# Delta rule with two pairs' token halves exchanged, and SSM decays as one product of 512 columns

## The reference

```python
def step(s, inp):
    r_t, w_t, k_t, v_t, kk_t, a_t = inp
    sa = jnp.einsum('bhvk,bhk->bhv', s, -kk_t)
    s = (s * w_t[:, :, None, :] + sa[..., None] * (kk_t * a_t)[:, :, None, :]
         + v_t[..., None] * k_t[:, :, None, :])
    return s, jnp.einsum('bhvk,bhk->bhv', s, r_t)
```

```python
a_cum = jnp.cumsum(dt * a.reshape(G, hg), axis=2)
seg = a_cum[:, :, :, None] - a_cum[:, :, None]
lmat = jnp.exp(jnp.where(mask, seg, -jnp.inf))
y_diag = jnp.einsum('bcqsgh,bcsghp->bcqghp', cb[..., None] * lmat, xdt)
```

## Time and profile before

| | |
|---|---|
| median of 3 runs | 3658.43 us |
| the profiled execution | 3661.18 us |
| its span, first to last instruction | 3659.9 us |
| TensorE busy, matmul / weight load | 3473.9 us (95%) / 2884.4 us (79%) |
| VectorE busy | 2100.5 us (57%) |
| ScalarE busy | 1330.3 us (36%) |
| mean granted TensorE clock | 0.976 |
| matmul records | 23320 |

### The profile page before, as it was taken

The page is one execution under the profiler, slowest core; times in us unless marked ns, Lnnn a source line. Parts: engine busy times, 40 slices in busy tenths (PEclk is TensorE's granted clock), DMA queues, the critical chain, the costliest instruction groups (busy, mean ns, idle before and its releaser), DMA issues.

```text
span 3659.9 us, 55917 instructions
## 1 busy us (share of the span) xinstructions
PE 3473.9 (95%) x23320; PEld 2884.4 (79%) x23320; DVE 2100.5 (57%) x3889; ACT 1330.3 (36%) x2454; POOL 65.0 (2%) x32
## 2 busy tenths in 40 slices
PE   7999999999999999999999988998999989889999
PEld 6777688788888777788788877786888778778887
DVE  6777643543457776535544467754655589573434
ACT  4456443342234555433332222222322234232222
POOL 0000000000000000000000000000000033000000
PEclk9999999999999999999999989999999999889999
DMA  4221223233333221233333332234100324233332
GB/s 133 81 62 50 58 76 110 81 99 97 98 125 92 74 61 52 64 97 100 88 97 98 104 89 73 83 95 137 29 29 21 116 70 135 84 115 92 98 98 87
DMA packets 353826, 315.36 MB, mean 86 GB/s; under 512 B 11348, under 2 KB 281812, under 8 KB 353576
## 3 DMA queue, kind: packets, MB, share of 16 engines
q1 hardware_dynamic: 352712, 309.56, 28.3%
q10 hardware_dynamic: 864, 2.23, 0.2%
HBM read 288.15 MB, written 23.59 MB: 85 GB/s over the span
## 4 chain that ended last, share of the span: by engine, by line
PE 77%; DVE 15%; ACT 5%; issue 3%; DMA 1%; POOL 0%; DVEq 0%; ACTq 0%; SPq 0%; POOLq 0%
PE banks L508 12%; PE banks L510 12%; PE banks L509 12%; PE banks L411 8%; PE banks L413 8%; PE banks L412 8%; PE banks L2578 6%; DVE weights_r L352 2%; PE banks L3000 2%; PE banks L608 1%; ACT weights_high_r L345 1%; PE banks L1091 1%; PE banks L1078 1%; ACT probabilities L1227 1%; DVE softmax_stats L1259 1%
## 5 line engine op out<-in xcount | busy, mean ns | idle before, releaser
L352 DVE TENSOR_TENSOR weights_r<-weights,weights_high_r 128x1024 fp32r<-128x1024 f32 (+3 forms) x520 | 606.6, 1174 | 478.5 <-ACT weights_high_r L345 477.8
L508 PE MATMUL banks<-h_T_hi,weights_high_r 128*128 128x512 f32 (+2 forms) x1904 | 759.7, 399 | 29.9 <-DVE h_T_lo L855 15.2
L510 PE MATMUL banks<-h_T_hi,weights_r 128*128 128x512 f32 (+2 forms) x1904 | 738.0, 388 | 0.0
L509 PE MATMUL banks<-h_T_lo,weights_high_r 128*128 128x512 f32 (+2 forms) x1904 | 737.8, 387 | 0.0
L345 ACT ACTIVATE weights_high_r<-weights 128x1024 fp32r<-128x1024 f32 (+3 forms) x520 | 510.4, 992 | 388.8 <-DMA weights<-in_w_mlp 217.9
L508 PEld LDWEIGHTS banks<-h_T_hi,weights_high_r 128*128 128x128 f32 x1904 | 362.9, 191 | 116.1 <-issue 38.0
L510 PEld LDWEIGHTS banks<-h_T_hi,weights_r 128*128 128x128 f32 x1904 | 362.2, 190 | 72.0
L509 PEld LDWEIGHTS banks<-h_T_lo,weights_high_r 128*128 128x128 f32 x1904 | 363.2, 191 | 69.0 <-issue 3.2
L411 PE MATMUL banks<-weights_high_r,h_T_hi 128*128 128x512 f32 (+3 forms) x704 | 290.5, 413 | 13.1 <-DVE h_T_lo L855 9.4
L413 PE MATMUL banks<-weights_high_r,h_T_lo 128*128 128x512 f32 (+3 forms) x704 | 266.6, 379 | 0.0
L412 PE MATMUL banks<-weights_r,h_T_hi 128*128 128x512 f32 (+3 forms) x704 | 266.4, 378 | 0.0
(11 more groups left out here) (541 smaller groups left out, 5643.6 us busy)
## 6 DMA issues: line engine op xcount, KB each, us to landing
weights<-in_w_in SPq DMA_DIRECT2D x182, 512.0 KB, 3.8
weights<-in_w_mlp SPq DMA_DIRECT2D x128, 512.0 KB, 3.8
weights<-in_ffn_w_in SPq DMA_DIRECT2D x44, 512.0 KB, 3.8
weights<-in_w_out SPq DMA_DIRECT2D x24, 512.0 KB, 3.6
weights<-in_ffn_w_down SPq DMA_DIRECT2D x22, 512.0 KB, 3.3
weights<-in_w_mem_kv SPq DMA_DIRECT2D x16, 512.0 KB, 3.6
weights<-in_w_diff_o SPq DMA_DIRECT2D x16, 512.0 KB, 4.0
weights<-in_w_mla_o SPq DMA_DIRECT2D x8, 512.0 KB, 3.4
```

Source lines behind the costliest of these rows:

```text
L352: ve.e.tensor_tensor(self.part(c.w_raw_r, u), self.part(c.w_raw, u), self.part(c.w_high_r, u).bitcast(F32), ALU.subtract).then_inc(*ve.tel ...
L508: pe.e.matmul(out, lhsT=wh[:, k, :], rhs=hi[k][:, cols], start=(k == 0), stop=False)
L509: pe.e.matmul(out, lhsT=wh[:, k, :], rhs=lo[k][:, cols], start=False, stop=False)
L510: mm = pe.e.matmul(out, lhsT=wl[:, k, :], rhs=hi[k][:, cols], start=False, stop=(k == self.chunks - 1))
```

## The change

In the delta rule the two halves of pairs f = 2 and 3 are exchanged in all tiles whose rows are tokens (low, w, cut, the six further products' tiles, x and sa). A product between a feature tile and a token tile then goes from one half of the partitions to the other for these two pairs. Inside the levels `cut` and `w` are exchanged, `t` and `prod` are not, so `prod` and `w step` cross for pairs 2 and 3, and `t step` does not. The initial `t` is masked from a product of its own, "low t", and not from `low`. `multiply` stays for products that don't cross. `crossing` and `swapping` issue the pairs in the order 0, 2, 1, 3 and write pairs 0, 1 to one bank and pairs 2, 3 to another; `fill_two` hands out two banks of the ring with one mark for when they are free, and a bank that would part the two at the ring's end is kept for the next single product. Some products share two banks (low with w, bu with rb, vtok with btok). The six further products move from one in each half level to 2, 2, 1, 1 ahead of levels 1 to 4. x and y are split in a straight part and a crossing part that adds to it.

```diff
+    def crossing(self, name, n, d, *terms, start=True):
+        pe, (together, at, _) = self.c.pe, self.SHARED[name]
+        if at == 0 and (together, n, d) not in self.two:
+            self.two[(together, n, d)] = self.two_banks(together, n, d)
+        for f in (0, 2, 1, 3):
+            for k, (lhsT, rhs) in enumerate(terms):
+                for rows in range(2):
+                    own, other = (slice(x % 2 * RC, (x % 2 + 1) * RC) for x in (rows, rows + f // 2))
+                    right = rhs[own, :] if len(rhs.shape) == 2 else rhs[own, f, :]
+                    mm = pe.e.matmul(self.two[(together, n, d)][f // 2][other, (2 * at + f % 2) * RC:(2 * at + f % 2 + 1) * RC],
+                                     lhsT=lhsT[own, f, :], rhs=right, start=start and k == 0,
+                                     stop=k == len(terms) - 1 and (start or f % 2 == 1))
+        mm.then_inc(*pe.tell("filled", name, n, d))
+    def two_banks(self, *key):
+        c = self.c
+        if (c.turns["scans"] + 1) % 6 == 0:
+            self.spare.append(c.next_of("scans"))
+        return c.fill_two(*key, ring="scans")
...
         pe.wait_ge("scaled_key", n, d)
-        self.multiply(("low", n, d), (o["a"], u["b"]))
-        self.multiply(("w", n, d), (u["b"], o["a"]))
+        self.crossing("low", n, d, (o["a"], u["b"]))
+        self.crossing("w", n, d, (u["b"], o["a"]))
+        self.multiply(("low t", n, d), (o["a"], u["b"]))
         yield
         pe.wait_ge("scaled_all", n, d)
-        fill = [("bu", (u["k"], o["a"])), ("vtok", (self.v[:, :, tc], i64)), ("rb", (u["b"], o["r"])), ("btok", (u["b"], i64)),
-                ("rk", (u["k"], o["r"])), ("ktok", (u["k"], i64))]
+        more = {1: (("vtok", (self.v[:, :, tc], i64)), ("btok", (u["b"], i64))), 2: (("bu", (u["k"], o["a"])), ("rb", (u["b"], o["r"]))),
+                3: (("ktok", (u["k"], i64)),), 4: (("rk", (u["k"], o["r"])),)}
         for lev in range(1, 6):
-            if fill:
-                name, term = fill.pop(0)
-                self.multiply((name, n, d), term)
+            for name, term in more.get(lev, ()):
+                self.crossing(name, n, d, term)
             yield
             pe.wait_ge("cut", n, d, lev)
             pe.wait_ge("w_level", n, d, lev - 1)
-            self.multiply(("prod", n, d, lev), (u["cut"], o["w"]))
-            if fill:
-                name, term = fill.pop(0)
-                self.multiply((name, n, d), term)
+            self.swapping(("prod", n, d, lev), u["cut"], o["w"])
             yield
             pe.wait_ge("emptied", "prod", n, d, lev)
             pe.wait_ge("t_level", n, d, lev - 1)
-            self.multiply(("w step", n, d, lev), (u["t"], u["prod"]))
+            self.swapping(("w step", n, d, lev), u["t"], u["prod"])
             if lev < 5:
                 self.multiply(("t step", n, d, lev), (u["prod"], u["t"]))
...
+        self.straight("x", n, d, (o["bu"], o["vtok"]))
...
-        self.multiply(("x", n, d), (o["a"], u["z"]), (o["bu"], o["vtok"]))
+        pe.wait_ge("straight", "x", n, d)
+        self.crossing("x", n, d, (o["a"], u["z"]), start=False)
...
-        self.multiply(("state", n, d), (o["btok"], u["sa"]), (o["ktok"], o["vtok"]))
-        self.multiply(("y", n, d), (u["z"], o["r"]), (u["sa"], o["rb"]), (o["vtok"], o["rk"]))
+        self.crossing("state", n, d, (o["btok"], u["sa"]), (o["ktok"], o["vtok"]))
+        pe.wait_ge("straight", "y", n, d)
+        self.crossing("y", n, d, (u["sa"], o["rb"]), (o["vtok"], o["rk"]), start=False)
```

```diff
-            for j in range(4):
-                mm = pe.e.matmul(bank[:, j * P:(j + 1) * P], lhsT=u["lhs"][q % 2][:, j * P:(j + 1) * P], rhs=k.upto[d], start=True, stop=True)
-            mm.then_inc(*pe.tell("filled", "ssm decay", d, n, q))
+            pe.e.matmul(bank[:, :], lhsT=k.strict[d], rhs=u["terms"][q % 2], start=True, stop=True).then_inc(*pe.tell("filled", "ssm decay", d, n, q))
```

Three plan times move:

```diff
-        P_.beside(cross, 238.5, 284.5, 0.38)
+        P_.beside(cross, 238.25, 284.25, 0.38)
...
-        plan.beside(rule, plan.now + 18, plan.now + 63.24, 1.08)
+        plan.beside(rule, plan.now + 18, plan.now + 63.37, 1.02)
...
-        plan.at(FirstGates(merge_h), (plan.now - 2,))
+        plan.at(FirstGates(merge_h), (plan.now - 1.62,))
```

More of the change, by code:

```diff
@@ L2572, in multiply @@
         c, pe = self.c, self.c.pe
-        bank = c.fill(*key, ring="scans")
+        bank = c.fill(*key, bank=self.spare.pop(0) if self.spare else c.next_of("scans"))
         for f in range(self.pairs):
@@ new lines, in two_banks, with swapping @@
+    def two_banks(self, *key):
[3 more added lines that the diff above has]
+        return c.fill_two(*key, ring="scans")
+    def swapping(self, key, lhsT, rhs):
+        c, pe = self.c, self.c.pe
+        two = self.two_banks(*key)
+        for f in (0, 2, 1, 3):
+            for rows in range(2):
+                own, other = (slice(x % 2 * RC, (x % 2 + 1) * RC) for x in (rows, rows + f // 2))
+                mm = pe.e.matmul(two[f // 2][other, f % 2 * RC:(f % 2 + 1) * RC], lhsT=lhsT[own, f, :], rhs=rhs[own, f, :],
+                                 start=True, stop=True)
+        mm.then_inc(*pe.tell("filled", *key))
@@ new lines, in swapped, with straight @@
+    def swapped(self, *key):
+        return self.c.slots[key][:, :, 0:2 * RC].rearrange("p b (f s) -> p b f s", f=2)
+    def straight(self, name, n, d, *terms):
+        pe, (together, at, _) = self.c.pe, self.SHARED[name]
+        if at == 0 and (together, n, d) not in self.two:
+            self.two[(together, n, d)] = self.two_banks(together, n, d)
+        for f in range(self.pairs):
+            for k, (lhsT, rhs) in enumerate(terms):
+                for own in (slice(0, RC), slice(RC, P)):
+                    mm = pe.e.matmul(self.two[(together, n, d)][f // 2][own, (2 * at + f % 2) * RC:(2 * at + f % 2 + 1) * RC],
+                                     lhsT=lhsT[own, f, :], rhs=rhs[own, f, :], start=k == 0 and f % 2 == 0, stop=False)
+        mm.then_inc(*pe.tell("straight", name, n, d))
@@ new lines, in shared, with wait_taken, wait_written @@
+    def shared(self, name, n, d):
+        together, at, _ = self.SHARED[name]
+        return self.c.slots[(together, n, d)][:, :, 2 * at * RC:(2 * at + 2) * RC].rearrange("p b (f s) -> p b f s", f=2)
+    def wait_taken(self, lane, name, n, d):
+        together, _, last = self.SHARED[name]
+        lane.wait_ge(*(("emptied", together) if last else ("taken", name)), n, d)
+    def wait_written(self, lane, name, n, d):
+        lane.wait_ge("filled", {"low": "w", "bu": "rb", "vtok": "btok"}.get(name, name), n, d)
@@ L2582, in got, with halves, taken @@
+    def halves(self, x):
+        return x.rearrange("p (b f) s -> p b f s", b=2)
+    def taken(self, lane, name, n, d):
+        together, _, last = self.SHARED[name]
+        return lane.frees(together, n, d) if last else lane.tell("taken", name, n, d)
     def got(self, *key):
@@ L2629, in copy @@
                     ac.wait_ge("filled", "y", n - 2, d)
-                ac.e.activation(o[name], self.got(name, n, d), ACT.Copy).then_inc(*ac.frees(name, n, d))
+                ac.e.activation(self.halves(o[name]), self.shared(name, n, d), ACT.Copy).then_inc(*self.taken(ac, name, n, d))
         for lev in range(1, 6):
-            if fill:
-                copy(fill.pop(0))
+            for name in {1: ("vtok", "btok"), 3: ("ktok",)}.get(lev, ()):
+                copy(name)
             yield
@@ L2691, in prepare_dve @@
             ve.e.tensor_tensor(u["cut"], u["low"], wide(k.level64[1 - d][lev]), ALU.mult).then_inc(*ve.tell("cut", n, d, lev))
-            if fill:
-                mask(*fill.pop(0))
+            for what in masks.get(lev, ()):
+                mask(*what)
             yield
-            if fill:
-                mask(*fill.pop(0))
             yield
             ve.wait_ge("filled", "w step", n, d, lev)
-            ve.e.tensor_tensor(w, w, self.got("w step", n, d, lev), ALU.subtract).then_inc(*ve.frees("w step", n, d, lev))
+            ve.e.tensor_tensor(halves(w), halves(w), self.swapped("w step", n, d, lev), ALU.subtract).then_inc(*ve.frees("w step", n, d, lev))
             c.values[("w_level", n, d, lev)] = ve.end
```

80 lines of the change are left out of this document (47 added, 33 removed).

## The result

The changed kernel takes 3629.9 us (median of 4 runs, 3628.0 to 3632.8) where the kernel before took 3658.5 on the same chip: a ratio of 0.9916, 95% interval 0.9904 to 0.9928. That is 29 us faster; the forecast was 42. The profiled execution took 3631.3 us, its span is 3630.0.

A forecast was written before the change was run, and what follows sets the result against it. TensorE was taken to bound the delta rule's stage, though not by much. From the 3658.43 us median, 41 us off the rule (36 + 4.5 + 0.5) and 1 off the SSM decays gave 3616; range 3600 to 3672.

The forecast's parts named there:

- TensorE's share: Sign in the delta rule's stage: TensorE's busy share should fall from 94% to some 85%.
- the distance of x to x: Sign, one chunk of the delta rule: over 38 us would make the prediction wrong.
- The waits for the cut: Sign at the rule's matmuls: waits for VectorE's cut should rise from 11 us.
- Price of a crossing product: Delta rule on TensorE: 0.26 us instead of 0.467, about 0.39 a term with two terms; saves 60 us of TensorE.
- the lower bound: Delta rule on TensorE: all four corners in step, 0.234 us a term everywhere, saving 78 us of TensorE.
- The rival of serial loads: Delta rule on TensorE: loads of one row half go serially, price stays 0.467 us, kernel slower at 3671; chance 0.21.
- the floor on starts: TensorE: about 25 ns between starts, so no term under 0.40 us, result near 3650; no separate chance given.
- Chunk 0 and the end: Delta rule's ends: preparation of chunk 0 saves 4.5 us, the last step 0.5 us.
- Net 5.2 us of a 40 us chunk: Delta rule's chunks: saving left after 0.6 us given back to bank waits; seven chunks give 36 us.
- The granted clock: Delta rule's stage: half speed in a tenth of it, 14 us less work done, giving 3630; no separate chance given.
- SSM decays: SSM scan: 8 records of 128 columns become 2 of 512, saving 1 us, bounds -1.5 and +1.
- cross and FirstGates: Layers' cross attention and hgrn gates, issue times moved: only queue places change, taken at 0, bounds -2 and +5.

The follow-up runs named there:

- e7: Kernel after with the pairs of crossing products issued in order 0, 1, 2, 3 instead of 0, 2, 1, 3; ratio 0.9925 to the kernel before.
- the second profile: Profile of the kernel after, run again unchanged as a control; ratio 0.9913 to the kernel before, stage 288.4 us.
- e6: Kernel after with the three plan times of before (cross, the rule, FirstGates) put back; 3639.0 us, ratio 0.9939 to the kernel before.
- the two repeats: Second runs of the unchanged kernel after (ratio 0.9913 to the kernel before) and of e9 (0.9901).
- e1: Kernel after with nothing exchanged, so every delta rule product stays in two corners, the rest of the rewrite kept; ratio 1.0022 to the kernel before.
- e13: Kernel after with the cut half a level earlier, further products behind prod and x's straight parts first, together; ratio 0.9904 to the kernel before.
- e9: Kernel after with both directions' straight part of x issued before the first crossing part; ratio 0.9897 to the kernel before, 0.9901 when repeated.
- e2: Kernel after with the SSM decays as four matmuls of 128 columns again, as before; ratio 0.9920 to the kernel before.

## Why the prediction was right in its sign and 13 us short

The range of 3600 to 3672 took in the rivals too, so that the time lies in it proves little, and its nearness is in part luck: TensorE's price came out better than forecast and the plan times may have helped, while the chunks gave little more than half. Of the signs that were named, the price (0.23 us), TensorE's share (86% for 85%) and the distance of x to x (37.0 us, under 38) came. The waits for the cut fell instead of rising, and the stage was 292.9 us at a clock of 0.98 instead of 278 at 1.00.

**Price of a crossing product: mechanism right, size at the bound.** 0.26 us and 0.39 a term of two were forecast, 0.23 and 0.23 to 0.24 came. "I take the corners to be independent in load and stream, but each to keep order" failed in its second half (e7). By these prices TensorE's saving is the 78 us of the lower bound, not 60. The rival of serial loads, and the floor on starts, are refuted by the first timeline above: 16 records in 0.23 us. Of the two pages the trace sides with "TensorEngine Tiling (Array Packing)" of the Trainium skill, Key Properties.

**Chunk 0 and the end: right for chunk 0, small at the end.** From the stage's start to the first x 32.1 us became 27.4, 4.7 less for 4.5 forecast; behind the last x 8.2 became 6.6, 1.6 less for 0.5.

**"Net 5.2 us of a 40 us chunk": this step failed.** It was 2.9, and 3.6 in the second profile. Seven chunks gave 20 us instead of 36, more than the whole difference of 13. By level, from the starts of VectorE's subtraction of `w step` of direction 0 (line 2699 before, 2786 after), mean of seven chunks, us:

| from, to | before | after | gained | forecast |
|---|---|---|---|---|
| x to level 1 | 17.70 | 15.83 | 1.87 | 1.57 + 0.7 |
| level 1 to 2 | 6.29 | 6.28 | 0.01 | 0.92 - 0.6 |
| level 2 to 3 | 4.87 | 3.21 | 1.66 | 1.57 |
| level 3 to 4 | 4.58 | 6.22 | -1.64 | 0.06 |
| level 4 to 5 | 4.77 | 4.09 | 0.68 | 0.4 |
| level 5 to x | 1.67 | 1.35 | 0.32 | - |

(the 0.6 for streamed units, forecast for all levels, is not in the rows; the 0.68 of level 4 to 5, which has a unit, holds part of it.) The chain worked out for a level holds where nothing else comes in: 3.15 us in most chunks for the 3.1 of level 3. The bank wait of level 2 is 1.07 us a chunk where 0.6 was taken; level 1 to 2 still took only 5.87 to 5.99 us in six of seven chunks (mean before 6.29); the seventh, 8.59, holds a stop of 0.98 us and a stretch at half clock. The mis-sized term is level 4. At its best, 5.15 us with a streamed unit of 1.4, it is 3.75 without, for 3.38 before and 3.4 forecast: the further product rk, its bank and its mask cost 0.37 more than was counted. In six chunks of seven it lasted longer, 5.4 to 8.4 us.

**What it was in those chunks: TensorE stands still in the middle of a product.** In five of the six such a stop lies in level 4. VectorE's subtractions in the last chunk but one, and TensorE's matmuls there and in the last chunk:
```profile
2800.67 0.42 DVE L2786 TENSOR_TENSOR cellsM<-cellsM,banks 128x256 f32<-128x256 f32 x1 [0.94 <-PE banks L2635]
2803.34 0.41 DVE L2786 TENSOR_TENSOR cellsX<-cellsX,banks 128x256 f32<-128x256 f32 x1
2807.03 0.42 DVE L2786 TENSOR_TENSOR cellsM<-cellsM,banks 128x256 f32<-128x256 f32 x1 [1.16 <-PE banks L2635]
```
```profile
2800.89 0.40 PE L2616 MATMUL banks<-cellsM,cellsE 64*64 64x64 f32 x11
2802.63 0.27 PE L2616 MATMUL banks<-cellsM,cellsE 64*64 64x64 f32 x2 [1.34 <-issue]
...
2836.29 0.22 PE L2616 MATMUL banks<-cellsS,cellsE 64*64 64x64 f32 x1
2838.47 0.40 PE L2616 MATMUL banks<-cellsS,cellsE 64*64 64x64 f32 x12 [1.97 <-issue]
```
A product of one term waits for semaphores before its first matmul only, so a stop behind its 13th record, or its first, is no wait for data. The stop of 1.34 us is what parts the subtractions at 2800.67 and 2803.34, where 1.11 us part those of the level before (2797.49 and 2798.60). Three things in the traces say that it is the supply of instructions.

The places: counted in TensorE's matmul records from the stage's start (the first is record 0), the stops of over 0.5 us that fall inside a product come behind records 2123, 2627, 3385, 4648, 5658, 6290, 6668 and 7678, eight in all; 2627, 4648 and 5658 are among them in e6, e7 and the two repeats as well. All distances are multiples of 126.3 (504 is 4, 758 is 6, 1263 is 10, 1010 is 8, 632 is 5, 378 is 3). With as many weight loads these are 252 instructions, and the few that signal besides.

The transfers: the instruction queue moves blocks of 16384 bytes, 64 in the stage, as many as it has 126s of records (8182 / 126 = 65). Over the whole kernel before it moves 186 such blocks for 2 x 23320 matmuls and loads of TensorE, 251 a block. By the Trainium skill, "Trainium Architecture — The Big Picture", The software stack, an instruction has 64 bytes; by it a block is 256 of them, which agrees. The transfers in 2638.0 to 2640.8 us of the kernel after:
```profile
q8 instruction: 1, 0.02, 2.1%
```
That block starts at 2638.37 us, and a stop ends at 2640.70. Every such stop ends 2.2 to 2.9 us after the start of the last block, and a block moves in 0.9 to 1.4 us.

The control: e1 has the same instructions in the same order, and no such stop; nor has before. At two corners 126 records last 126 / 16 x 0.467 = 3.7 us, at four 1.84, which is less than the 2.2 to 2.9. So at four corners TensorE can run out of instructions, and the less it waits for anything else, the oftener: 4.2 to 11.1 us in the other kernels at four corners, 15.5 in e13. No kernel was run that changes the supply alone (fewer instructions for the same products), so the link from block to stop rests on the traces.

**The granted clock: foreseen as a rival, and a part of the loss.** Both stages begin at half speed (1.2 GHz), before for 4 us and after for 3. Beyond that it is at half speed for 10 us of the stage of after, in three pieces, and never in the stage of before. Windows of the kernel after, with the clock in the third column from the right:
```profile
2596.00:2600.00 4.00, 2.06 (x72) 1.65 (x68) 4.00 (x11) 0.57 (x3) 0.00 (x0) 1.00 0.00 0
2602.00:2603.00 1.00, 1.00 (x38) 1.00 (x38) 0.88 (x3) 0.00 (x0) 0.00 (x0) 0.50 0.00 0
...
2836.00:2838.00 2.00, 0.51 (x18) 0.43 (x14) 1.18 (x3) 0.10 (x1) 0.00 (x0) 1.00 0.00 0
2840.00:2842.00 2.00, 2.00 (x8) 1.61 (x6) 0.75 (x3) 0.00 (x0) 0.00 (x0) 0.52 0.00 0
```
Each piece follows a stretch in which TensorE stood still for much of the time: 2.06 of 4 us busy behind a weight split on VectorE, 0.51 of 2 at the stop of 1.97 us, and the stop of 0.98 at 2686. At half speed 10 us do the work of 5. Beyond its beginning the second profile has one piece of 3.4 us and a stage 4.5 us shorter, e13 none; so the clock doesn't explain why e13 is no faster.

**The wait that was not foreseen.** The crossing part of x waits for the straight part that it adds to: 0.35 us beyond the pace, in 16 places, and e9 clears them all. For y the state's product stands between the two parts, and the crossing part starts without a wait. The 15 further waits behind a straight part that the expectation of e9 counts are that state product's, 0.34 or 0.62 us from record to record; by the trace they mostly end with VectorE's read of a bank, and no run moved them.

**The other edits: right within what can be told.** SSM decays -1 us: where nothing waits, the next product mostly starts 0.86 or 0.91 us after a decay, where it was 0.89 or 0.95, so 0.03 to 0.04 a decay came, as forecast; e2 can't tell it from 0 in the time. cross and FirstGates taken at 0 with bounds of -2 and +5; the third plan time, the rule's own density, was not priced at all. e6 says that the three together may be worth some 10 us, a gain that the sum had nowhere; it fell below the forecast all the same because of the chunks. The price of the change without the crossing, +13 in the rival, is +8.

## What to carry to other kernels

Where small fp32 products use only two of four quarters of the array, send every second pair across: loads and streams of all four run at once, which halves the product (here 0.47 to 0.23 us), and alternate the quarters in the order of issue. Then ask at once what is next: here 78 us less of TensorE, by the price, gave a stage 27 to 31 us shorter. The rest went to the chain through the other engines and to stops for which only the instruction supply is left as a reason; they came where 126 matmul records take 1.84 us, and not where they take 3.7. Before clearing a wait, see whether TensorE also stops inside products, where no semaphore can hold it.

## What the hardware showed that was not expected

- Four quarters load and multiply at once in fp32: 16 records in 0.23 us, 32 in 0.49.
- TensorE's instructions come in blocks of 16 KB for 126 matmul records; with 1.84 us of work in a block it stopped for over 0.5 and up to 2.0 us, eight and seven times in the two profiles of the kernel after, always at distances that are a multiple of 126 records. That the supply is the cause is read from these traces, not shown by a run of its own. With 3.7 us in a block it never did.
- In a stage where TensorE is busy 86% of the time, the granted clock fell to half for 3.4 us three times, after stops of 0.98 and 1.97 us and after 4 us in which it was busy for 2.06.
- Two executions of the kernel after differ by 5.1 us before the rule even begins (2563.6 and 2558.5 us), with 116 and 89 us at half clock up to there (their spans differ by 8.4).
